# PEER pass as one stretch: gates of one half of the second keys built between the U or V blocks of the other half

## What is computed

```python
PEER_HEADS = 8; PEER_DK = 128; N_KEYS = 128; N_EXPERTS = N_KEYS * N_KEYS; PEER_TOPK = 16
def one(t):                                   # 128 tokens of width 1024
    q = (t @ wq).reshape(TOKEN_BLOCK, PEER_HEADS, 2, PEER_DK // 2)
    s = jnp.einsum("thpd,hpnd->thpn", q, sub_keys).astype(jnp.float32)
    st, it = lax.top_k(s, PEER_TOPK)
    cand = (st[:, :, 0, :, None] + st[:, :, 1, None, :]).reshape(TOKEN_BLOCK, PEER_HEADS, PEER_TOPK * PEER_TOPK)
    cidx = (it[:, :, 0, :, None] * N_KEYS + it[:, :, 1, None, :]).reshape(...)
    best, pos = lax.top_k(cand, PEER_TOPK)
    e = jnp.take_along_axis(cidx, pos, axis=-1)
    g = jax.nn.softmax(best, axis=-1)
    u = jnp.take(eu, e, axis=0)
    act = jax.nn.gelu(jnp.einsum("thkd,td->thk", u, t).astype(jnp.float32), approximate=False)
    return jnp.einsum("thk,thkd->td", (g * act).astype(ev.dtype), jnp.take(ev, e, axis=0))
```

## Time and profile before

| | us |
|---|---|
| median of 3 runs | 4712.65 (4710.53 to 4717.93) |
| profiled execution, its own time | 4713.23 |
| its span | 4711.4 |
| PE busy | 4159.6 (88%) |
| POOL busy | 1889.7 (40%) |
| DVE busy | 2038.5 (43%) |
| ACT busy | 1807.0 (38%) |

### The profile page before, as it was taken

How to read it: one execution, slowest core, us unless ns; L and a number is a source line. 1 busy time by engine, 2 the same in 40 slices (tenths; PEclk the granted TensorE clock), 3 DMA queues, 4 the chain that set the end, 5 groups by cost and what they waited for, 6 DMA issues and landing times. The chain is left out here.

```text
span 4711.4 us, 69166 instructions
## 1 busy us (share of the span) xinstructions
PE 4159.6 (88%) x23266; PEld 3473.4 (74%) x23266; DVE 2038.5 (43%) x4396; ACT 1807.0 (38%) x2885; POOL 1889.7 (40%) x1373
## 2 busy tenths in 40 slices
PE   7998899978767999779989996999796789987998
PEld 7953379865433999768879995788674589976886
DVE  4012422164532872356640005666456281035665
ACT  4522104132212455653335546433322155565333
POOL 6830008132000888960018879200130088886000
PEclk9998899988578999789999997899895799987999
DMA  5564445411001555115545550355320245521554
GB/s 189 180 205 161 164 138 168 154 64 54 3 27 58 164 172 172 66 63 188 187 159 183 182 183 5 117 187 187 103 93 3 68 148 174 182 77 39 188 187 147
DMA packets 168891, 611.15 MB, mean 130 GB/s; under 512 B 18448, under 2 KB 21648, under 8 KB 168464
## 3 DMA queue, kind: packets, MB, share of 16 engines
q1 hardware_dynamic: 168720, 608.87, 39.3%
HBM read 606.70 MB, written 2.10 MB: 129 GB/s over the span
## 5 line engine op out<-in xcount | busy, mean ns | idle before, releaser
L1655 POOL TENSOR_TENSOR ring_r<-ring,ring_hi 128x1024 fp32r<-128x1024 f32 x384 | 971.3, 2536 | 187.9 <-ACT ring_hi L1727 187.0
L1688 PE MATMUL bank<-H_r,ring_hi 128*128 128x256 f32 x3072 | 876.1, 285 | 44.6 <-POOL ring_r L1655 44.6
L1689 PE MATMUL bank<-H_r,ring_hi 128*128 128x256 f32 x3072 | 871.9, 284 | 0.0
L1690 PE MATMUL bank<-H_r,ring_r 128*128 128x256 f32 x3072 | 871.7, 284 | 0.0
L276 POOL TENSOR_TENSOR ring_r<-ring,ring_hi 128x1024 fp32r<-128x1024 f32 x183 | 446.1, 2442 | 662.8 <-ACT ring_hi L270 662.6
L1961 ACT ACTIVATE ring_hi<-ring 128x1024 fp32r<-128x1024 f32 x384 | 407.3, 1062 | 690.0 <-DMA ring<-in_peer_v 649.1
L1688 PEld LDWEIGHTS bank<-H_r,ring_hi 128*128 128x128 f32 x3072 | 592.3, 193 | 51.5 <-issue 24.6
L1689 PEld LDWEIGHTS bank<-H_r,ring_hi 128*128 128x128 f32 x3072 | 592.6, 193 | 0.0
L1690 PEld LDWEIGHTS bank<-H_r,ring_r 128*128 128x128 f32 x3072 | 592.4, 193 | 0.0
L2009 PE MATMUL bank<-ring_hi,w_parts 128*128 128x512 f32 x1536 | 485.9, 397 | 10.4 <-DVE ring_r L1976 10.4
L2011 PE MATMUL bank<-ring_r,w_parts 128*128 128x512 f32 x1536 | 484.8, 397 | 0.0
(11 more groups left out here) (317 smaller groups left out, 6060.4 us busy)
## 6 DMA issues: line engine op xcount, KB each, us to landing
ring<-in_peer_u SPq DMA_DIRECT2D x384, 512.0 KB, 3.5
ring<-in_peer_v SPq DMA_DIRECT2D x384, 512.0 KB, 3.5
ring<-in_w_in SPq DMA_DIRECT2D x135, 512.0 KB, 3.5
ring<-in_ada SPq DMA_DIRECT2D x96, 512.0 KB, 4.5
ring<-in_w_f SPq DMA_DIRECT2D x72, 512.0 KB, 3.5
ring<-in_w_br SPq DMA_DIRECT2D x24, 512.0 KB, 3.5
ring<-in_w_out SPq DMA_DIRECT2D x16, 512.0 KB, 3.5
ring<-in_w_q SPq DMA_DIRECT2D x16, 512.0 KB, 3.4
```

What stands on the lines that cost most here:

```text
L1655: pool.tensor_tensor(ring_lo[:, slot, :], ring[:, slot, :], ring_hi[:, m % NH, :].bitcast(F32), ALU.subtract).then_inc(p_lo, 1)
L1688: pe.matmul(o, hi[:, k], x_hi_[:, kt, :], start=(kt == 0), stop=False)
L1689: pe.matmul(o, hi[:, k], x_lo_[:, kt, :], start=False, stop=False)
L1690: mm = pe.matmul(o, lo[:, k], x_hi_[:, kt, :], start=False, stop=(kt == KT - 1))
```

## The change

The list `small_columns` loses the lambda parameters; they come by a DMA of their own (128 x 256 numbers) at the start of each layer, and DVE waits for it. The gains of the norms are written over the modulation table instead of a tile of their own. For each stream there is now an RMS norm of its own that also leaves the tokens split in high and rest, and then one `Phase` for everything up to the last V block:

- `w_q` is streamed for each stream and multiplied in three parts like a U block (eight more blocks of 24 matmuls, POOL making the rest); `spill` is gone.
- Scores of two tiles between the first U blocks; search on DVE during the first 64 U blocks, for this stream's two tiles alone.
- The gates are built in 64 groups of 8 tokens by 64 second keys: 32 groups for the second keys 0 to 63 between the U blocks 64 to 127 (a group ahead of every two blocks), and 32 groups for the second keys 64 to 127 between the V blocks 0 to 63. A group is 8 matmuls with 64 columns (before: 4 with 128). DVE alone makes both one-hot matrices (8 rows with weights, one instruction for the columns) and applies the gates. ACT and POOL have no part in it any more.
- The rests of the V blocks 0 to 63 are made by POOL, those of 64 to 127 by DVE as before. ACT's high parts go on as before.

```diff
             order += [(w_in2[l], i) for i in range(25)]
             order += [(w_out2[l], i) for i in range(8)]
-            order += [(w_q2[l], i) for i in range(8)]
             for _ in range(2 if l == 0 else 1):
+                order += [(w_q2[l], i) for i in range(8)]
                 order += [(peer_u[l], i) for i in range(NK)]
                 order += [(peer_v[l], i) for i in range(NK)]
...
+                    sp.dma_start(lamt, lam[l]).then_inc(lam_in, 16)
+                    dve.wait_ge(lam_in, 16)
...
+            for s in streams:
+                A.at = 0
+                x_hi_, x_lo_ = H_r[:, :, 1 - s, :], H_r[:, :, s, :]
+                rms_phase(norm_jobs(32, 24, (s,)), lambda j, kt: (x_hi_[:, kt, :], x_lo_[:, kt, :]))
+
+                R = A.take(3, T)
+                S = A.take(NK, T)
+                hotA = A.take(2, 8, P)
+                hotB = A.take(2, 8, NK // 2)
...
+                        with pool.Fori(0, 16) as it:
+                        for m in range(192, v0 + HALF):
...
+                        def build(g, it=None):
+                            n = g if it is None else it * 6 + g
+                            pe.wait_ge(v_hot, n + 1)
+                            if it is not None or g not in (0, 1, 32, 33):
+                                pe.wait_ge(v_g, n - 1)
+                            o = bank[(0 if g < 32 else 4) + g % 2]
+                            for u in range(8):
+                                mm = pe.matmul(o[:, u * 64:(u + 1) * 64], hotA[:, g % 2, u, :], hotB[:, g % 2, u, :],
+                                               start=True, stop=True)
+                            mm.then_inc(g_ps, 1)
...
+                            pe.wait_ge(p_lo if c < HALF else v_lo, turns(it, m + 1 if c < HALF else c - HALF + 1))
+                            pe.wait_ge(v_w, turns(it, c + 1))
...
+                        build(0)
...
+                        with pe.Fori(0, 5) as it:
+                            for i in range(6):
+                                build(2 + i, it)
+                                up(68 + 2 * i, it)
+                                up(69 + 2 * i, it)
+                        pe.wait_ge(a_gelu, NK)
...
+                        with pe.Fori(0, 5) as it:
+                            for i in range(6):
+                                build(34 + i, it)
+                                down(4 + 2 * i, it)
+                                down(5 + 2 * i, it)
+
+                        with pe.Fori(0, 5) as it:
+                            for i in range(12):
+                                down(HALF + i, it)
+                        for c in range(HALF + 60, NK):
...
+                        def hot(g, it=None):
+                            if g >= 2:
+                                dve.wait_ge(g_ps, g - 1 if it is None else it * 6 + (g - 1))
+                            t = 8 * (g % 32) if it is None else it * 48 + 8 * (g % 32)
+                            for u in range(8):
+                                dve.tensor_scalar(hotA[:, g % 2, u, :], cc("iota"), rows_[:, bass.ds(t + u, 1)],
+                                                  wts[:, bass.ds(t + u, 1)], ALU.is_equal, ALU.mult)
+                            second = cc("iota")[:, 64 * (g // 32):64 * (g // 32) + 64]
+                            dve.tensor_tensor(hotB[:, g % 2, :, :], second.unsqueeze(1).to_broadcast([P, 8, 64]),
+                                              cols_[:, bass.ds(t, 8)].unsqueeze(2).to_broadcast([P, 8, 64]),
+                                              ALU.is_equal).then_inc(v_hot, 1)
+
+                        def gate(g, it=None):
+                            dve.wait_ge(g_ps, g + 1 if it is None else it * 6 + (g + 1))
+                            t = 8 * (g % 32) if it is None else it * 48 + 8 * (g % 32)
+                            first = 64 * (g // 32)
+                            w = S[:, first:first + 64, bass.ds(t, 8)]
+                            o = bank[(0 if g < 32 else 4) + g % 2][:, :].rearrange("p (t k) -> p k t", t=8)
+                            dve.tensor_tensor(w, w, o, ALU.mult).then_inc(v_g, 1)
...
+                        dve.wait_ge(a_t, TT)
+                        hot(0)
+                        hot(1)
+                        dve.wait_ge(a_gelu, HALF)
+                        with dve.Fori(0, 5) as it:
+                            for i in range(6):
+                                gate(i, it)
+                                hot(i + 2, it)
+                        gate(30)
+                        hot(32)
+                        gate(31)
+                        hot(33)
+                        dve.wait_ge(v_g, 32)
+                        dve.wait_ge(blocks_done, n0 + v0)
+                        dve.wait_ge(a_gelu, NK)
+
+                        with dve.Fori(0, 5) as it:
+                            for i in range(6):
+                                split(2 * i, it)
+                                split(2 * i + 1, it)
+                                gate(32 + i, it)
+                                hot(34 + i, it)
+                        for i in (30, 31):
+                            split(2 * i)
+                            split(2 * i + 1)
+                            gate(32 + i)
+                        dve.wait_ge(v_g, 64)
+
+                        with dve.Fori(0, 5) as it:
+                            for i in range(12):
+                                split(HALF + i, it)
+                                low(HALF + i, it)
...
-                    groups = T // 4
...
-                                hot = pool.tensor_scalar(hotB[:, 4 * (g % 4) + u, :], cc("iota"),
-                                                         cols_[:, 4 * g + u:4 * g + u + 1], None, ALU.is_equal)
...```

On DVE, in the gate stage of the first pass before (line 1903 makes a row with weight, line 1909 applies a group to `S`; ISA and REGISTER_ALU are address arithmetic):

```order
L1903 TENSOR_SCALAR H<-CS,arena 128x128
L1903 ISA
L1903 TENSOR_SCALAR H<-CS,arena 128x128
L1907 REGISTER_ALU
L1909 ISA
L1909 TENSOR_TENSOR arena<-arena,bank 128x128x4
```

475 lines of the change are left out of this document (166 added, 309 removed).

## The result

The changed kernel takes 4729.53 us (median of 7 runs, 4722.91 to 4735.44), the kernel before in the same session 4714.55 (4709.31 to 4719.62): ratio 1.0031, 95% interval 1.0021 to 1.0041. It is slower, by a third of a percent. The profiled execution took 4728.25 us, 15.0 more than that of before (4713.23). The forecast of 4706 was 22 us too low, its range held the time, and its sign was wrong.

What follows compares the result with a forecast made beforehand. TensorE bounds the U and V stages, POOL's column instructions layer 1's gate stage. Three passes sum to 2880.3 us, 11.4 less than 2891.7; with 4.4 for lambda parameters, 4713.2 becomes 4706 us. Range 4640 to 4835.

Steps and rivals of the forecast that it cites:

- Where TensorE was to be the bound: U and V stages: TensorE busy all the time, 2.89 us a U block, 2.82 us a V block.
- Gates on TensorE: Each group of gates: 16 matmul halves at 0.112 us whatever their columns, 1.8 us of TensorE.
- Gates on VectorE: Rows, columns and gate product 3.4 us a group; with two splits 4.75 us a V pair.
- U pair: U blocks 64 to 127: VectorE with POOL's turns 7.05 to 7.7 us, TensorE 7.6; taken as 7.7.
- V pair of blocks 0 to 63: VectorE the bound: 4.75 us work plus 4.3 in turns, less part of the gate product; taken as 8.8.
- The third: Rival, slower: each turn costs the whole subtraction, 8.2 us a U pair, 9.6 a V pair, total 4831; chance 0.20.
- The fourth: Rival: the clock falls in the V half as TensorE idles, or an unseen wait; some hundred us more; chance 0.05.
- the first: Likeliest case: turns cost as said, 8.3 to 9.1 us a V pair, total 4648 to 4744; chance 0.60.
- signs against me: Would show the forecast wrong: among others, V blocks 0 to 63 over 300 us, or granted clock below 0.95.
- The second: Rival: POOL does not hold VectorE up, TensorE bounds both halves, 134 us less, total 4572; chance 0.15.
- V blocks 64 to 127: Second half of V in each pass: 64 blocks at 2.82 us, 180.5 us.
- Lambda parameters: Small transfer at each layer's start: 2.2 us each, 4.4 us in all, or 0 if covered.

Runs made afterwards that it cites:

- splits_ahead: Changed kernel with four buffers for the split gates instead of two, VectorE making the splits one pair ahead: 4642.58 us, ratio 0.9849 to the kernel before.
- rest_timed: Changed kernel with POOL starting the rests of the next V pair only behind both splits of this one: 4639.17 us, ratio 0.9844 to the kernel before.
- gate_between: Changed kernel with the gate product between the two splits of a pair, not behind both: 4758.68 us, ratio 1.0079 to the kernel before.
- the four kernels that reach it: Changed kernel with V 0 to 63 rests left out, both or one a pair on VectorE, or rows reading PSUM: 4523.2, 4525.52, 4523.78, 4531.11 us.
- rests_dve: Changed kernel with VectorE, not POOL, making all rests of V blocks 0 to 63: 4525.52 us, ratio 0.9602 to the kernel before.
- rests_one: Changed kernel with the second rest of each V pair made by VectorE, the first by POOL: 4523.78 us, ratio 0.9599 to the kernel before.
- rest_halves: Changed kernel with POOL making each rest of V blocks 0 to 63 in two subtractions of 512 columns: 4636.89 us, ratio 0.9844 to the kernel before.
- build_narrow: Changed kernel with gate matmuls of 32 columns instead of 64, half of the gates left out: 4707.0 us, ratio 0.9984 to the kernel before.

## Why the prediction was wrong

Added up over three passes, in us (predicted, measured): norm, first block and result 74.1, 77.6; q and U blocks 0 to 63 680.7, 676.4; U 64 to 127 739.2, 724.5; V 0 to 63 844.8, 899.4; V 64 to 127 541.5, 521.5. The sum is 2899.4 against 2880.3, and 7.7 more than before the change. Outside the passes 7.3 came on top, 4.4 expected.

- **Where TensorE was to be the bound: right.** It is busy without a gap in both U halves but for the search (217.6 of 225.9 us) and in V 64 to 127, as in the earlier trace rows; the search is over in time (225.9 us for the half with it, 226.9 predicted).
- **Gates on TensorE: right.** 16 halves take 1.8 us, by the count of matmuls; the run with 32 columns shows that it is so beyond what the rows of before had.
- **Gates on VectorE: right.** 4.75 us a pair in V predicted, 4.60 measured.
- **U pair: right within 2%.** 7.7 predicted, 7.53 measured, in every pair: TensorE's own time. VectorE has 2.5 us to spare, for only one of POOL's two subtractions meets work there: in 234 us some 32 turns of 1.7 us beside 62 subtractions. The bound by VectorE that I took doesn't exist there.
- **V pair of blocks 0 to 63: the step that failed.** I took VectorE's work plus its turns, 4.75 + 4.3, less part of the gate product, 8.8 us, as if VectorE never stood. Measured 9.54 (9.44 and 9.33 in the passes before, first group's gates to the last's): 55 us over three passes, more than the whole error of 22. It was not the turns: 3.38 us, below my 4.3. The term that was missing is 1.57 us in which VectorE waits for TensorE. A turn on a split that TensorE is waiting for stops TensorE, the lower clock follows on the stop, and the late block starves VectorE and POOL alike. On TensorE's side the 2.28 us over 7.26 are 1.42 of standing and 0.86 of the same matmuls taking longer (248.63 of 292 us busy is 8.12 a pair). That the place of the turn makes the idle time is shown; how much of the 1.57 us comes of the stop and how much of the clock was not separated. Three runs without that idle time (`splits_ahead`, `rest_timed`, the regular stretch of `gate_between`) took 8.53, 8.50 and 8.25 us a pair: about what I had predicted for a bound by VectorE's work and turns.
- **The forecast of the total was near by luck.** 4706 is 22 us from the profiled 4728, though the terms were off by 59 us one way and 39 the other, because these largely cancelled.
- **The rivals.** The third (slower, each turn the whole subtraction; where the prediction speaks of the skill's rule it calls this one the second) named this place: at 9.6 us a pair in V, and with waits that begin late as its reason. Its pair was met, by another sum (it had whole turns and no idle time), and its U half was not. The fourth, the clock, I had priced at some hundred us and 0.05 and set apart from the first; the granted clock of 0.92 in the V half, and the 303 us of that half in the third pass, are what I had written down as signs against me. They were no rivals but one chain. The second, no hold-up and TensorE the bound, was put at 4572; the four kernels that reach it take 4523 to 4531.
- **V blocks 64 to 127: 20 us too high.** A block takes 2.72 us (173.80 for 64) where the earlier trace rows had 2.82. The records of the same matmuls are 389 ns long against 395, at the full clock in both. The splits lie in another buffer than before; whether that is the reason wasn't tried.
- **Lambda parameters: as said**, up to the size. VectorE waits 2.7 and 2.3 us for the small transfer at the start of the two layers, and the phase is some 1.5 us longer than before; 4.4 for two was the upper bound. The other 4 us outside the passes lie in code that the change doesn't touch.
- **The sign.** The terms missed by -20, -15, -4, +4 and +55; with 96 pairs a tenth of a microsecond in one term is worth half of the band that separates faster from slower. I had put 0.44 on slower and 0.39 on faster.

`rests_dve` and `rests_one` beat both kernels by 4%. The change is worth that once POOL is kept out of the V half; VectorE had room for both rests all along, 6.83 us of work in a pair against TensorE's 7.26.

## What to carry over

When VectorE and GpSimd both work on SBUF beside TensorE, don't add the turns to the busiest engine's sum alone: ask for each turn who waits for the instruction that it can hit, and keep the instruction that feeds TensorE clear of it, by giving the work to VectorE where it has room, by reading one operand from PSUM, by working one buffer ahead, or by letting GpSimd start behind it. A stop of TensorE of 3 us or more cost a second time here, at the lower clock behind it, each time; stops of 1 us and less seldom did in most of these kernels and nearly always in one, so look at the granted clock behind the stop and don't go by its length. Before moving an instruction in such a loop, draw the loop through both engines once round with its sum.

## What the runs showed of the hardware

- `tensor_scalar` with two pointers and its source in PSUM isn't held by GpSimd: eight in 2.63 us across a subtraction of 2.39; with the source in SBUF 4.20.
- The price of a turn is what is left of the other's instruction: 1.5 to 2.0 us on average for a subtraction of 2.4, 0.9 for one of 1.35. Cutting the instruction in two left the sum at 3.3 us a pair and took away two thirds of the idle time.
- Over three passes each, blocks that ran slow (3.6 us or more from first to last matmul, the others 2.7 or less) behind stops of TensorE ahead of a V block: changed kernel, 3.0 to 3.3 us, 33 of 33 (granted clock 0.57 in the one shown), 0.59 to 0.85 us, 0 of 21; `gate_between`, 2.6 to 2.9 us, 25 of 30, under 0.95 us, 0 of 61; `rest_halves`, 2.0 to 2.3 us, 11 of 15; `rest_timed`, 0.89 to 1.15 us, 8 of 79. Against these `build_narrow`: 0.78 to 0.87 us, 22 of 25.
- A loop of these two engines can have two steady patterns with one code, 8.25 and about 10 us a pair (`gate_between`), and change between them within an execution; that kernel's total spread over 48 us from run to run.
